# One projection of both branches, seven products per pair, in a stage of its own

## The chip, the cores and the metric

The kernel runs on one core of one Trainium2 chip. The metric is the device time of one execution in microseconds (us).

## The reference

`x` has 4096 rows of 1024 features. `h = RMSNorm(x)` goes through one projection (`w_in`, 1024 to 3072 columns). Its first 1024 columns feed the pooling branch: causal window means of 2, 4, 8 and 16 rows minus the value, mixed by a 128x128 matrix per group of 128 columns, times a SiLU gate. The other 2048 feed the attention branch: 8 heads of 64, chunks of 64 rows that each read themselves and eight chunks before, a relative-position bias, softmax, times a SiLU gate. Both branches (512 columns each) are concatenated; the part that the change rebuilds is

```
y = jnp.concatenate([y_pool, y_attn], axis=-1)
x = x + jnp.einsum('bse,ed->bsd', y, w_out[layer])
return rms_norm(x, final_norm_gain)
```

All tensors are float32. The kernel splits each operand of a product into a high and a low float16 part and makes three matmuls for one (high x high, high x low, low x high).

## The kernel before, in words

Rows are handled in 32 blocks of 128, in 16 pairs of 256 rows. One instruction stream per engine is written out by hand; each stream is in order, and `wait_ge` blocks everything behind it on that engine. SyncE (SP) issues almost all transfers from one such stream.

- **Stage 1** (`h_phase_*`): norm, transposes, and projection of values and gates. Most pairs are made with seven products of quarter matrices (Winograd's form of Strassen's scheme) in place of eight. The split operands of every pair go to memory (`h_ops`).
- **Stage 2** (`q_phase_*`): the pooling branch, 8 tiles `t` of 512 rows, each with 4 steps `k`; a step `m = 4t + k` is one window group and has 7 products of 12 matmuls of 256 columns (L1108 to L1111). VectorE (DVE) combines them (`take_*`, L1248), builds windows (`level`, L1307), and `scale_gate(m - 1)` (L1329, count `y_done`) makes the branch output of step m-1 during step m, after `take_c22(m)`. In the loop, ScalarE (ACT, `y_hi`) and GpSimd (POOL, `y_lo`) split it. TensorE (PE) then multiplies it with the pooling half of `w_out` (`output`, L1132) beside the next tile's products: 2, 2 and 4 outputs of 12 matmuls of 512 columns behind steps 1, 2 and 3. DVE adds `x` (`residual`, L1339), and SP stores the sum as `residual` in memory. `load_hop` (L1072) fetches the seven operands of tile t+1 into one buffer, each behind the wait for its last use in step 3 of tile t. `load_wk` (L1478) fetches pieces of the key and query weights; steps 8, 11, ..., 29 begin a piece, which POOL, ACT (L1207) and DVE (L1352) turn into operands. Outputs of the last tile stand in the passage to stage 3.
- **Stage 3** (`a_phase_*`): attention, 16 tiles of 256 rows, 8 heads each. Each head has three places (`other`, slots 3h to 3h+2) where PE does other work beside the softmax chain: slots 0 to 6 take query products of the tile to come, slots 7 to 16 the attention half of the output of tile t-1 (`output`, L1936), slots 17 to 23 key products (L1701 to L1704, 24 matmuls of 128 columns each). ACT makes exponentials (L2086) and high parts (L2092), POOL low parts (L2263). DVE adds the residual (L2192); ACT squares (L2101), POOL takes the root, DVE scales (L2201), SP stores the result.

Of the kernel before, what the change touches and what calls it, by code (L numbers as in the profile page):

```python
# [20 lines left out]
P = 128  # L21
# [84 lines left out]
def build(nc, x, norm_gain, w_in, pool_w, pool_scale, rel_fwd, rel_rev, w_out, final_gain, out):  # L106
# [7 lines left out]
    r_dram = nc.dram_tensor("residual", (BLOCKS, P, D), F32, kind="Internal").ap()  # L114
# [5 lines left out]
    with ctx:  # L120
# [58 lines left out]
        yp_h = view(Z, 19712, (2, NKT, PT), F16)  # L179
        yp_l = view(Z, 27904, (2, NKT, PT), F16)  # L180
        xres = view(E, 0, (2, D), F32)
        wot_h = view(E, 8192, (NKT, D), F16)
        wot_l = view(E, 16384, (NKT, D), F16)
# [11 lines left out]
        junk3 = view(RM, 40128, (D,), BF16)  # L195
# [4 lines left out]
        res = view(E, 0, (2, D), F32)  # L200
        res_last = view(RM, 43008, (2, D), F32)
        wob_h = view(E, 8192, (NKT, D), F16)
        wob_l = view(E, 16384, (NKT, D), F16)
# [8 lines left out]
        yT_h = view(Z, 34048, (NKT, AT), F16)  # L212
        yT_l = view(Z, 36096, (NKT, AT), F16)
# [697 lines left out]
        def h_phase_sp(sp):  # L911
# [86 lines left out]
        names = """psc_done mm p1_done u_done c11_done tanh_done z_done step_done y_done yh_done yl_done op_mm r_done  # L998
            wk_loaded wk_sums wk_hi wk_lo wot_hi wot_lo h_over""".split()
        Q = {n: sem("q_" + n) for n in names}  # L1000
        wot_loaded = [sem(f"q_wot_loaded{n}") for n in range(NKT)]
        entry_loaded = [sem(f"q_entry_loaded{s}") for s in range(PRODUCTS)]
        hop_loaded = [sem(f"q_hop_loaded{s}") for s in range(PRODUCTS)]
        xres_loaded = [sem(f"q_xres_loaded{s}") for s in range(2)]
        r_stored = [sem(f"q_r_stored{s}") for s in range(2)]

        pj6 = psum[0:6]
        op = [wide[:, 0:512], wide[:, 512:1024]]
        LASTM = GROUPS * PTILES - 1

        ENDBLK = PBLK * PTILES - 2

        def op_bank(n, n2):

            return psum[1 - n2][:, :] if n >= ENDBLK else op[n2]

# [36 lines left out]
        def wot_stage(n):  # L1053

            if n == 2:
                return wst2.rearrange("p a b c d -> p (a b c d)")
            return xres[:, min(n, 1), :]

# [16 lines left out]

        def wot_at(m):

            return {GROUPS: (0,), GROUPS + 1: (1, 2), GROUPS + 2: (3,)}.get(m, ())

        def q_phase_pe(pe):  # L1080
# [33 lines left out]
            def output(t, b, n2):  # L1114

                n = PBLK * t + b
                if b == 0 and n2 == 0:
                    pe.wait_ge(Q["yl_done"], GROUPS * t + GROUPS)
                    if t == 0:
                        pe.wait_ge(Q["wot_lo"], NKT)  # L1120
                        pe.wait_ge(H["t_done"], 4 * PAIRS)
                        pe.wait_ge(H["hlo_done"], 3 * PAIRS)
                        pe.wait_ge(H["b12_done"], b12_at(PAIRS - 1))
                if n == ENDBLK:
                    pe.wait_ge(A["kq_u"], 5 * 3)
                elif n > 0:
                    pe.wait_ge(Q["r_done"], 2 * n - 1 + n2)
                for kt in range(NKT):
                    yh = yp_h[:, t % 2, kt, b * P:(b + 1) * P]
                    yl = yp_l[:, t % 2, kt, b * P:(b + 1) * P]  # L1130
                    for part, w in ((yh, wot_h), (yh, wot_l), (yl, wot_h)):
                        mm = nc.tensor.matmul(op_bank(n, n2), part, w[:, kt, n2 * 512:(n2 + 1) * 512],  # L1132
                                              start=(kt == 0 and w is wot_h and part is yh),
                                              stop=(kt == NKT - 1 and part is yl))
                mm.then_inc(Q["op_mm"], 1)
# [11 lines left out]
            for b in range(2):  # L1147
                for n2 in range(2):
                    output(PTILES - 1, b, n2)
# [3 lines left out]
            for x in range(4):  # L1153
                first_maxima(pe, x)
                output(PTILES - 1, 2 + x // 2, x % 2)


        def outputs_after(t, k):

            if t == 0:  # L1160
                return ()
            if t == 1:
                return range(PBLK) if k == GROUPS - 1 else ()
            return ((), (0,), (1,), (2, 3))[k]

        def q_phase_act(act):
# [6 lines left out]
            def copy_c11(m):  # L1173
                act.wait_ge(Q["mm"], PRODUCTS * m + 5)
                at_least(act, Q["yl_done"], m - 1)
# [9 lines left out]

            def y_hi(m):
                t, k = m // GROUPS, m % GROUPS
                act.wait_ge(Q["y_done"], m + 1)
                if m == 0:
                    act.wait_ge(Q["h_over"], 1)  # L1190
                if k == 0 and t > 1:
                    act.wait_ge(Q["op_mm"], 2 * PBLK * (t - 1))
                nc.scalar.activation(yp_h[:, t % 2, GORDER[k], :], vb[:, m % 2, HIST:], ACT.Copy).then_inc(Q["yh_done"], 1)  # L1193

            def wot_hi(n):
                act.wait_ge(wot_loaded[n], 16)
                nc.scalar.activation(wot_h[:, n, :], wot_stage(n), ACT.Copy, scale=WS).then_inc(Q["wot_hi"], 1)
# [13 lines left out]
            for m in range(GROUPS * PTILES):  # L1211
                copy_p1(m)
                if m > 0:
                    gate_tanh(m - 1)
                for n in wot_at(m):
                    wot_hi(n)
# [4 lines left out]
                if m > 0:  # L1221
                    y_hi(m - 1)
            gate_tanh(LASTM)
            kq_copy_p1(act, 0)
            y_hi(LASTM)
# [9 lines left out]
        def q_phase_dve(dve):  # L1235
# [33 lines left out]
            def take_c12(m):  # L1269
                dve.wait_ge(Q["mm"], PRODUCTS * m + 6)  # L1270
                at_least(dve, Q["yl_done"], m - 1)
# [61 lines left out]
            def residual(t, b, n2):  # L1333

                n = PBLK * t + b
                dve.wait_ge(Q["op_mm"], 2 * n + n2 + 1)
                dve.wait_ge(xres_loaded[b % 2], 16 * (2 * t + b // 2 + 1))
                cols = slice(n2 * 512, (n2 + 1) * 512)
                nc.vector.scalar_tensor_tensor(  # L1339
                    out=xres[:, b % 2, cols], in0=op_bank(n, n2), scalar=1.0 / (WS * YS), in1=xres[:, b % 2, cols],  # L1340
                    op0=ALU.mult, op1=ALU.add).then_inc(Q["r_done"], 1)

            def wot_lo(n):
                dve.wait_ge(Q["wot_hi"], n + 1)
                nc.vector.scalar_tensor_tensor(
                    out=wot_l[:, n, :], in0=wot_stage(n), scalar=WS, in1=wot_h[:, n, :],
                    op0=ALU.mult, op1=ALU.subtract).then_inc(Q["wot_lo"], 1)

# [7 lines left out]
            for m in range(GROUPS * PTILES):  # L1356
# [16 lines left out]
                for n in wot_at(m):  # L1373
                    wot_lo(n)
# [8 lines left out]
                for b in outputs_after(t, k):  # L1383
                    for n2 in range(2):
                        residual(t - 1, b, n2)
# [1002 lines left out]
```

## Time and profile before

| | us |
|---|---|
| median of 3 runs (lowest, highest) | 1660.24 (1659.97, 1664.46) |
| profiled execution, device time | 1663.83 |
| its span | 1662.0 |
| TensorE busy | 1615.7 (97% of the span) |
| VectorE busy | 1064.2 (64%) |
| ScalarE busy | 839.0 (50%) |
| GpSimd busy | 667.6 (40%) |

Busy times are unions over an engine's overlapping instructions: a matmul of 512 columns is recorded with 379 ns, although the next one starts sooner. Pitch must therefore be read from starts. The mean granted clock of TensorE was 0.994 of full speed. Stage 1 ends at about 360 us, stage 2 at about 805 us, attention runs from about 857 us.

### The profile page before, as it was taken

What the parts mean: (1) busy time and instruction counts of PE and PEld (TensorE: products, weight loads), DVE (VectorE), ACT (ScalarE), POOL (GpSimd) and SP (SyncE); (2) the same over time, 40 slices, a digit from 0 to 9 for tenths busy, and PEclk for the clock granted to TensorE, in tenths of its full rate; (3) what the DMA queues carried; (4) which work ended last, traced back from release to release, by engine and by line L of the source; (5) the groups of instructions that cost most, each with busy time, mean ns of one, the idle gap of its engine ahead of it and who ended that gap; (6) DMA issues with size and microseconds to landing.
All of it is one profiled execution on the core that took longest, in us unless ns stands there. A gap on an engine that the chain in (4) does not pass through costs nothing. (4 is left out here: it accounts for less than half of the span.)

```text
span 1662.0 us, 44366 instructions
## 1 busy us (share of the span) xinstructions
PE 1615.7 (97%) x17944; PEld 1219.2 (73%) x17944; DVE 1064.2 (64%) x2201; ACT 839.0 (50%) x1589; POOL 667.6 (40%) x718
## 2 busy tenths in 40 slices
PE   7899999999999999999999999999999999999997
PEld 3455455468677777767778988889888898888974
DVE  7877767747565565556346666666666666666665
ACT  6555555522111111112126776767767676776775
POOL 3443333311101111111414465555655555555564
PEclk9999999999999999999999999999999999999999
DMA  6656456473615533542765534444344443344341
GB/s 238 211 188 222 183 210 222 178 264 136 221 61 177 199 127 105 178 165 90 224 210 165 154 90 136 138 135 146 96 131 140 135 142 114 117 137 137 96 141 51
DMA packets 144001, 258.01 MB, mean 155 GB/s; under 512 B 16024, under 2 KB 77992, under 8 KB 141752
## 3 DMA queue, kind: packets, MB, share of 16 engines
q1 hardware_dynamic: 142760, 253.88, 46.1%
q8 instruction: 143, 2.34, 0.6%
q0 software_dynamic: 1040, 1.31, 0.5%
q14 instruction: 58, 0.48, 0.1%
HBM read 151.40 MB, written 83.54 MB: 141 GB/s over the span
## 5 line engine op out<-in xcount | busy, mean ns | idle before, releaser
L2263 POOL TENSOR_TENSOR stages<-stages 128x512 f16<-128x512 f32 (+2 forms) x368 | 363.9, 991 | 353.9 <-ACT stages L2092 353.6
L1701 PE MATMUL bank<-middle,weights 128*128 128x128 f16 x1792 | 311.5, 219 | 2.7 <-DVE entry L1339 2.7
L1704 PE MATMUL bank<-middle,weights 128*128 128x128 f16 x1792 | 311.5, 219 | 0.0
L1703 PE MATMUL bank<-middle,weights 128*128 128x128 f16 x1792 | 311.4, 219 | 0.0
L2086 ACT ACTIVATE stages<-bank,log_ps 128x512 f32<-128x512 f32 (+2 forms) x368 | 221.6, 602 | 158.6 <-PE bank L1959 97.5
L1906 DVE CUSTOM_DVE_ANT_0 stages<-bank,stages 128x640 bf16<-128x640 f32 (+4 forms) x256 | 198.6, 776 | 74.6 <-PE bank L1871 74.3
L1108 PE MATMUL bank<-middle 128*128 128x256 f16 x784 | 214.4, 274 | 3.5 <-DVE stages L1248 3.5
L1111 PE MATMUL bank<-middle 128*128 128x256 f16 x784 | 214.5, 274 | 0.0
L1110 PE MATMUL bank<-middle 128*128 128x256 f16 x784 | 214.4, 274 | 0.0
L2092 ACT ACTIVATE stages<-stages 128x512 f16<-128x512 f32 (+2 forms) x368 | 202.9, 551 | 11.7
L1936 PE MATMUL bank<-entry,stages 128*128 128x512 f16 x768 | 190.8, 379 | 1.1 <-DVE stages L2148 1.1
L1701 PEld LDWEIGHTS bank<-middle,weights 128*128 128x128 f16 x1792 | 175.5, 98 | 3.4 <-issue 3.2
L1703 PEld LDWEIGHTS bank<-middle,weights 128*128 128x128 f16 x1792 | 175.6, 98 | 0.6
L1704 PEld LDWEIGHTS bank<-middle,weights 128*128 128x128 f16 x1792 | 175.5, 98 | 0.0
L1132 PE MATMUL bank<-entry,stages 128*128 128x512 f16 x768 | 169.7, 379 | 0.5 <-DVE middle L1734 0.5
L1956 PE MATMUL bank<-middle 128*128 128x256 f16 (+1 forms) x840 | 162.4, 243 | 3.1 <-DVE middle L2180 1.7
L1414 POOL TENSOR_TENSOR stages<-stages 128x512 f16<-128x512 f32 x32 | 38.0, 1189 | 302.3 <-ACT stages L1193 302.3
L330 PE MATMUL bank<-weights,middle 128*128 128x512 f16 x392 | 148.8, 380 | 1.1 <-DVE stages L689 1.1
L332 PE MATMUL bank<-weights,middle 128*128 128x512 f16 x392 | 148.8, 380 | 0.0
L333 PE MATMUL bank<-weights,middle 128*128 128x512 f16 x392 | 148.7, 379 | 0.0
L1132 PEld LDWEIGHTS bank<-entry,stages 128*128 128x128 f16 x768 | 75.0, 98 | 86.1 <-DVE middle L1734 0.6
L1734 DVE SCALAR_TENSOR_TENSOR middle<-bank,middle 128x256 f32<-128x256 f32 x160 | 67.8, 424 | 102.6 <-PE bank L1704 101.4
(157 smaller groups left out, 3673.1 us busy)
## 6 DMA issues: line engine op xcount, KB each, us to landing
entry<-in_x SPq DMA_DIRECT2D x64, 512.0 KB, 3.8
h_ops<-middle SPq DMA_DIRECT2D x16, 1792.0 KB, 6.1
middle<-h_ops SPq DMA_DIRECT2D x112, 256.0 KB, 5.5
middle<-h_ops SPq DMA_DIRECT2D x49, 512.0 KB, 7.6
middle<-middle SPq DMA_DIRECT2D x384, 64.0 KB, 2.0
residual<-entry SPq DMA_DIRECT2D x32, 512.0 KB, 2.9
out<-entry SPq DMA_DIRECT2D x32, 512.0 KB, 2.7
entry<-residual SPq DMA_DIRECT2D x30, 512.0 KB, 4.9
```

Source lines behind the costliest of these rows:

```text
L1108: nc.tensor.matmul(bank, wh, hop[:, :, s, 0, kt, :], start=(kt == 0 and s < 4), stop=False, skip_group_check=True)
L1110: nc.tensor.matmul(bank, wh, hop[:, :, s, 1, kt, :], start=False, stop=False, skip_group_check=True)
L1111: mm = nc.tensor.matmul(bank, wl, hop[:, :, s, 0, kt, :], start=False, stop=(kt == 3), skip_group_check=True)
L1132: mm = nc.tensor.matmul(op_bank(n, n2), part, w[:, kt, n2 * 512:(n2 + 1) * 512], start=(kt == 0 and w is wot_h and part is yh), stop=(kt = ...
L1701: nc.tensor.matmul(dst, wh, hop3[:, o, 0, kt, :], start=(kt == 0 and s < 2 and pair == 0), stop=False, skip_group_check=True)
L1703: nc.tensor.matmul(dst, wh, hop3[:, o, 1, kt, :], start=False, stop=False, skip_group_check=True)
L1704: mm = nc.tensor.matmul(dst, wl, hop3[:, o, 0, kt, :], start=False, stop=(kt == 3), skip_group_check=True)
L1906: nc.vector.tensor_tensor_reduce((junk0 if t == 0 and h < 2 else junk2)[:, c:640], wide[:, c:640], bias_q[:, h, c:640], 1.0, -3e38, ALU.ad ...
L1936: mm = nc.tensor.matmul(out_bank(t, i), yh, w, start=(m == 0), stop=(m == 11))
L2086: nc.scalar.activation(p32[g][:, a:b], score_bank(g)[:, a:b], ACT.Exp, bias=log_ps[:, 0:1]).then_inc(A["exp_done"], 1)
L2092: nc.scalar.activation(p_h[:, h % 2, c + a:c + b], p32[g][:, a:b], ACT.Copy).then_inc(A["ph_done"], 1)
L2263: nc.gpsimd.tensor_tensor(p_l[:, h % 2, c + a:c + b], p32[g][:, a:b], p_h[:, h % 2, c + a:c + b], ALU.subtract).then_inc(A["pl_done"], 1)
```

## The change

Neither branch is multiplied with `w_out` where it is made. Stage 2 stores each step's output to a new tensor `branches` in memory (`store_y`, on SP), and stage 3 stores the transposed attention output (`store_branch`). All `output`, `residual`, `y_hi`/`y_lo` and `r_dram` transfers go. The slots 7 to 16 stay empty; the key products move to slots 9, 11, ..., 21. A fourth stage (`f_phase_*`) loads each pair's branch outputs (1 MB) and x (1 MB) and makes the output with seven products, all in float16 pairs as before. Pairs 0 and 1 take the plain eight; half of these (16 halves of 6 matmuls) fill slots of the last two attention tiles, for which weights and branch outputs are loaded and split there.

```diff
 # stage 2, SP
+            def store_y(m):
+                sp.wait_ge(Q["y_done"], m + 1)
+                sp.dma_start(y_dram[2 * (m // GROUPS):2 * (m // GROUPS) + 2, :, GORDER[m % GROUPS], :].rearrange("a p n -> p a n"),
+                             vb[:, m % 2, HIST:].rearrange("p (a n) -> p a n", a=2)).then_inc(y_stored[m % 2], 16)
...
             for t in range(1, PTILES):
                 for k in range(GROUPS):
                     m = GROUPS * t + k
-                    if t == 1 and k == 1:
-                        load_res(0)
+                    store_y(m - 1)
                     if t == 1 and k == GROUPS - 1:
-                        load_res(1)
                         load_wk(0)
                     i, parts = wk_at(m)
                     if parts and parts[0] == 0 and i > 0:
                         load_wk(i)
                     if k == GROUPS - 1 and t + 1 < PTILES:
                         for s in range(PRODUCTS):
                             load_hop(sp, t + 1, s)
...
-                    for b in outputs_after(t, k):
-                        n = PBLK * (t - 1) + b
-                        store_res(n)
-                        load_res(n + 2)
+            store_y(LASTM)
             load_v(sp, 0, 0)
             load_gate(sp, 0, 0)
             load_bias(sp)
 # stage 2, PE
             for m in range(GROUPS * PTILES):
-                t, k = m // GROUPS, m % GROUPS
                 for s in range(PRODUCTS):
                     product(m, s)
-                for b in outputs_after(t, k):
-                    for n2 in range(2):
-                        output(t - 1, b, n2)
 # stage 3
+        K_SLOTS = (9, 11, 13, 15, 17, 19, 21)
...
-            first = 9 if t == 0 else 17
-            return (2 * t + 4, x - first) if t + 2 < ATILES and first <= x < first + PRODUCTS else None
+            return (2 * t + 4, K_SLOTS.index(x)) if t + 2 < ATILES and x in K_SLOTS else None
...
+        PLAIN_SLOTS = tuple((t, h, a) for t, h in [(LAST - 1, h) for h in (6, 7)] + [(LAST, h) for h in range(6)]
+                            for a in (0, 2))
+        WEIGHT_AT = {(LAST - 1, 3): (0,), (LAST - 1, 4): (1,), (LAST, 1): (2,), (LAST, 5): (3,)}
+        PLAIN_AT = {(LAST - 1, 4): ((0, 0),), (LAST - 1, 5): ((0, 1),), (LAST, 0): ((1, 0),), (LAST, 2): ((1, 1),)}
...
+            if p == 0 and half == 0:
+                sp.wait_ge(A["nat_lo"], 2 * ATILES)
+                for r in range(2):
+                    sp.wait_ge(yt_stored[r], 32)
+            else:
+                sp.wait_ge(F["plain_lo"], 2 * p + half)
+            sp.dma_start(ys[:, :, :], y_dram[p, :, NKT * half:NKT * half + NKT, :]).then_inc(F["ys_loaded"], 16)
...
                 move_k(sp, t + 1, 0)
                 move_q(sp, t + 1, 0)
                 load_v(sp, t + 1, 0)
                 load_gate(sp, t + 1, 0)
+                if t == LAST - 1:
+                    load_x4(sp, 0)
+                    for p, half in ((0, 0), (0, 1), (1, 0)):
+                        load_plain(sp, p, half)
                 move_k(sp, t + 1, 1)
                 move_q(sp, t + 1, 1)
 # stage 4, PE and VectorE
+            for p in range(PLAIN):
+                for q in range(4, 8):
+                    for part in range(2):
+                        plain_half(pe, p, q, part)
+            for p in range(PLAIN, PAIRS):
+                for s in range(PRODUCTS):
+                    product(p, s)
...
+            for p in range(PLAIN, PAIRS):
+                more = p + 1 < PAIRS
+                take_u2(p)
+                take_u4(p)
+                if more:
+                    operand_lo(p + 1, 0)
+                    operand_lo(p + 1, 1)
+                finish(2 * p - 2, 2 * p - 1)
+                take_c22(p)
+                if more:
+                    sums(p + 1)
+                finish(2 * p - 1, 2 * p)
+                add_x(p, 1, 0, 1, 2)
+                add_x(p, 0, 1, 1, 2)
+                take_c11(p)
+                if more:
+                    operand_lo(p + 1, 2)
+                take_c12(p)
+                take_c21(p)
```

## Rows read from the trace of the kernel before

**Rows 1.** The page, busy time by engine and share of the span

```profile
PE 1615.7 (97%) x17944; PEld 1219.2 (73%) x17944; DVE 1064.2 (64%) x2201; ACT 839.0 (50%) x1589; POOL 667.6 (40%) x718
```

**Rows 2.** The page, costliest groups: busy us, mean ns of one | idle before

```profile
L1936 PE MATMUL bank<-entry,stages 128*128 128x512 f16 x768 | 190.8, 379 | 1.1 <-DVE stages L2148 1.1
...
L1132 PE MATMUL bank<-entry,stages 128*128 128x512 f16 x768 | 169.7, 379 | 0.5 <-DVE middle L1734 0.5
```

**Rows 3.** Timeline of PE at 603 us: start us, us, instruction

```profile
602.71 5.34 PE L1132 MATMUL bank<-entry,stages 128*128 128x512 f16 x24
607.89 0.27 PE L1108 MATMUL bank<-middle 128*128 128x256 f16 x1
```

**Rows 4.** Timeline of SP at 612 us (step 19)

```profile
611.81 5.80 SPq L1072 DMA_DIRECT2D middle<-h_ops  x7
```

**Rows 5.** Timeline of DVE at 613 us (step 19)

```profile
613.67 0.74 DVE L1329 SCALAR_TENSOR_TENSOR stages<-stages,psc 128x512 f32<-128x512 f32 x1
```

**Rows 6.** L1072, the transfer issued at 554.0 us

```profile
DMA to landing us min/median/max: 4.6/4.6/4.6
```

**Rows 7.** L1072, the transfer issued at 498.3 us, behind two of L1478

```profile
DMA to landing us min/median/max: 5.9/5.9/5.9
```

**Rows 8.** L1072, the last of seven, issued at 559.4 us

```profile
DMA to landing us min/median/max: 8.4/8.4/8.4
```

**Rows 9.** Timeline of SP at 634 us (step 20)

```profile
633.91 0.91 SPq L1478 DMA_DIRECT2D entry<-in_w_in  x2
```

**Rows 10.** Timeline of ACT from 634 us (step 20)

```profile
634.17 0.38 ACT L1176 ACTIVATE stages<-bank 128x256 f32<-128x256 f32 x1 [4.34 <-PE bank L1111]
638.39 1.03 ACT L1207 ACTIVATE weights<-entry 128x256 f16<-128x256 f32 x3 [3.83 <-DMA entry<-in_w_in]
```

**Rows 11.** Timeline of PE at 646 us, in brackets its idle time before

```profile
646.34 0.28 PE L1108 MATMUL bank<-middle 128*128 128x256 f16 x1 [3.03 <-DVE stages L1248]
```

**Rows 12.** Stretch behind it: busy PE, PEld, DVE, ACT, POOL, then granted clock, DMA

```profile
646.00:650.00 4.00, 3.66 (x22) 2.62 (x23) 3.57 (x8) 0.63 (x1) 0.66 (x1) 0.67 0.02 4
```

**Rows 13.** Timeline of ACT in the passage to attention

```profile
806.46 0.38 ACT L1711 ACTIVATE middle<-bank 128x256 f32<-128x256 f32 x1 [10.30 <-PE bank L1704]
...
859.38 0.38 ACT L1711 ACTIVATE middle<-bank 128x256 f32<-128x256 f32 x1 [9.23 <-PE bank L1704]
```

**Rows 14.** Timeline of SP in the passage to attention

```profile
819.41 8.18 SPq L1821 DMA_DIRECT2D middle<-middle  x12
```

**Rows 15.** L1768, the transfer issued at 827.6 us

```profile
DMA to landing us min/median/max: 3.2/3.2/3.2
```

**Rows 16.** Timeline of ACT: first exponentials of heads (14,0), (14,6), (14,7), (15,0)

```profile
1555.96 0.47 ACT L2086 ACTIVATE stages<-bank,log_ps 128x256 f32<-128x256 f32 x1 [1.82 <-PE bank L1959]
...
1593.57 0.47 ACT L2086 ACTIVATE stages<-bank,log_ps 128x256 f32<-128x256 f32 x1
...
1597.59 0.46 ACT L2086 ACTIVATE stages<-bank,log_ps 128x256 f32<-128x256 f32 x1
...
1603.21 0.47 ACT L2086 ACTIVATE stages<-bank,log_ps 128x256 f32<-128x256 f32 x1 [1.67 <-PE bank L1959]
```

**Rows 17.** The page, DMA issues: KB each, median us to landing

```profile
entry<-in_x SPq DMA_DIRECT2D x64, 512.0 KB, 3.8
```

**Rows 18.** Groups by line: DVE's work on an output bank and on rows

```profile
L2192 DVE SCALAR_TENSOR_TENSOR entry<-bank,entry 128x512 f32<-128x512 f32 x60 | 41.4, 690 | 23.3 <-PE bank L1936 23.0
...
L2201 DVE SCALAR_TENSOR_TENSOR entry<-entry,stat 128x1024 f32<-128x1024 f32 x30 | 38.7, 1289 | 0.0
```

**Rows 19.** Timeline of DVE, two of L1307 without and two beside POOL

```profile
539.49 1.44 DVE L1307 TENSOR_TENSOR stages<-stages 128x525 f32<-128x525 f32 x2
...
582.54 1.84 DVE L1307 TENSOR_TENSOR stages<-stages 128x525 f32<-128x525 f32 x2
```

**Rows 20.** Timeline at the end: last PE group, ACT's last square

```profile
1649.64 4.05 PE L1936 MATMUL bank<-entry,stages 128*128 128x512 f16 x18
...
1655.69 1.06 ACT L2101 ACTIVATE middle<-middle 128x1024 bf16<-128x1024 f32 x1 [1.38 <-DVE middle L2192]
```

More of the change, by code:

```diff
@@ L1490, in q_phase_sp @@
             sp.nop().then_inc(Q["h_over"], 1)
-            for n in range(NKT):
-                load_wot(n)
+            for m in range(GROUPS - 1):
+                store_y(m)
             for t in range(1, PTILES):
@@ L2128, in head @@
                 if round_at(t, h):
-                    branch_hi(*round_at(t, h))
+                    branch_copy(*round_at(t, h))
                 other(t, h, 2)
-                for of, j in squares_at(t, h):
-                    square(of, j)
-                if t == 0 and h in WOB_HEADS:
-                    wob_hi(WOB_HEADS.index(h))
+                for w in WEIGHT_AT.get((t, h), ()):
+                    for half in range(2):
+                        final_hi(act, w, half)
+                for p, half in PLAIN_AT.get((t, h), ()):
+                    plain_hi(act, p, half)
             max_row(0, 0)
@@ L2139, in a_phase_act @@
                     head(t, h)
[L2140 to L2142 removed]
+            branch_copy(LAST, 1)
         def a_phase_dve(dve):
[L2145 to L2151 removed]
             def add_bias(t, h):
@@ L2216, in other @@
                         kq_take(dve, w, KQ_TAKES[s])
-                for of, i, _, end in output_slot(t, h, a):
-                    if end == 12:
-                        residual(of, i)
             def head(t, h):
@@ L2231, in head @@
                     maximum(dve, t2, h2, 1)
-                if round_at(t, h):
-                    branch_lo(*round_at(t, h))
                 other(t, h, 2)
-                for of, j in finish_at(t, h):
-                    finish(of, j)
-                if t == 0 and h in WOB_HEADS:
-                    wob_lo(WOB_HEADS.index(h))
+                before_h = (t, h - 1) if h > 0 else (t - 1, HEADS - 1)
+                for w in WEIGHT_AT.get(before_h, ()):
+                    for half in range(2):
+                        final_lo(dve, w, half)
+                for p, half in PLAIN_AT.get(before_h, ()):
+                    plain_lo(dve, p, half)
+                if (t, h) in TAKE_AT:
+                    plain_take(dve, *TAKE_AT[t, h])
             for t in range(ATILES):
@@ new lines, in final_source, with final_dst, final_hi @@
+        def final_source(w, half):
+            if w < 4:
+                return raw4[w][:, 2 * half:2 * half + 2, :]
+            return (s2w, s1w, s3w, s1w)[w - 4][half][:, :, :]
+        def final_dst(w, part, half):
+            return w4[2 if w == 7 else w][:, part, 2 * half:2 * half + 2, :]
+        def final_hi(act, w, half):
+            if w < 4:
+                act.wait_ge(raw_loaded[w], 16)
+                if w == 0 and half == 0:
+                    act.wait_ge(A["kq_mm"], PRODUCTS * 2 * ATILES)
+            elif w in (5, 6):
+                act.wait_ge(F["s13_done"], 2 * (w - 5) + half + 1)
+            else:
+                act.wait_ge(F["sum_done"], (2 if w == 7 else 0) + half + 1)
+            if w == 4 and half == 0:
+                act.wait_ge(A["pv_mm"], HEADS * ATILES)
+                act.wait_ge(A["max_done"], 2 * HEADS * ATILES)
+            if w == 7:
+                act.wait_ge(F["plain_mm"], 15)
+                act.wait_ge(F["w_lo"], 6)
+            nc.scalar.activation(final_dst(w, 0, half), final_source(w, half), ACT.Copy, scale=WS).then_inc(F["w_hi"], 1)
@@ L2344, in _ @@
             a_phase_pe(pe)
+            f_phase_pe(pe)
         @block.scalar
```

754 lines of the change are left out of this document (417 added, 337 removed).

## The prediction

> **What bounds the kernel now.** I read the page's busy times first: TensorE (PE) is busy for 1615.7 of 1662.0 us, VectorE (DVE) for 64%, the others for half or less [rows 1]. So PE's work sets the time, and removing matmuls pays if no wait takes their place. Then I read its groups. Both outputs are 768 matmuls each, recorded with 379 ns [rows 2]; that is duration, not pitch. The pitch is in the starts: 24 matmuls begin at 602.71 and the next product at 607.89, so 5.18 / 24 = 0.216 us [rows 3]. Last I read the SyncE (SP) queue and whoever waits for a transfer, since the change rebuilds that queue. Today's outputs are PE work that needs nothing fresh, so they also hide the landing of what comes next.
>
> **Matmuls.** Before: 1536. After: 2 pairs x 96 + 14 pairs x 84 = 1368. 168 fewer at 0.216 us are **-36 us**. Everything below is a wait that PE has beside that.
>
> **Stage 2, operands of the next tile.** A step has 84 matmuls of 256 columns, 1.31 us a product, 9.2 us a step. `load_hop` can only start behind the products of step 3, and product s of the next tile follows 7.9 us after the release of its buffer. Today four outputs (10.4 us) lie between. They go. SP must now also pass `store_y(m-1)` first, which waits for `y_done`: step 19 starts at 607.89 [rows 3], and L1329 ends at 613.67 + 0.74 = 614.41, 6.5 us into the step [rows 5]; before, the first load was out at 611.81, 3.9 us in [rows 4]. With the store's issue the load goes out at about 7.1 and lands 4.6 later [rows 6], at 11.7; PE wants it at 9.2. The others follow some 1.3 apart (the last of seven issued at 559.4 landed at 567.8 [rows 8]), so nothing is caught up: 2.7 us for step 19. In steps 7, 11 and 23 two weight transfers go out ahead (0.9 us of queue, landing after 5.9 [rows 7]): 8.05 + 5.9 = 13.95, 4.9 us each. Steps 15 and 27 follow a late step (next part); their `y_done` comes at about 12, and I count 4.4 each. Sum 2.7 + 3 x 4.9 + 2 x 4.4 = **+26**. Bounds: 6 x 2.5 = 15 to 6 x 6 = 36.
>
> **Stage 2, key and query weights.** Their pieces (steps 11 to 29, every third) today mostly go out at a step's start. Once, in step 20, SP was held up: ACT's copy after product 4 starts at 634.17, so the step began at about 627.5; the transfers went out at 633.91, 6.4 in [rows 9]; ACT could start on them at 638.39 [rows 10]; DVE, in order, was late for everything behind, and in the next step PE waited 3.03 us [rows 11]. After the change each of these transfers is behind `store_y`, at 6.9 to 8.4. Where a longer window keeps DVE busier I add its delay: steps 14, 17, 20, 26, 29: 3.7, 5.0, 3.5, 3.7, 5.0 = 20.9, less 3.3 that is there today: **+18** (in 11 and 23 the operand wait covers it). Bounds 5 x 2 - 3.3 = 7 to 25.
>
> **Clock.** After the 3.03 us of waiting the granted clock averages 0.67 over the next 4 us [rows 12]: it fell from 2.4 to 1.2 GHz for part of it, and some 1.7 us of work came later. Ten of the new waits are longer than that one: 10 x 1.7 = 17; part overlaps what PE would wait for anyway, so **+13** (0 to 20).
>
> **Passage to attention.** 96 output matmuls (20.7 us) leave it. Query products began at 806.46 and again at 859.38 [rows 13], some 52.5 us after PE's start on them. SP's order is now binding: key moves from 819.41 take 8.2 us of issue [rows 14], only then come the operands of tile 1, first landing 3.2 us later [rows 15]: 25.7 us after the start, when PE has had nothing since 18.7. Seven products (9.4) and the first maxima (about 5, with a lowered clock) make 41. So 11.5 us are gained of 20.7: **+9**, and +2 for the same wait ahead of tile 0's operands. Bounds 4 to 18.
>
> **Attention, tiles 1 to 13.** Outputs leave every tile (10.4 us). ACT needs about 4.0 us a head: head (14,6), which has no filling, lasts 1593.57 to 1597.59 [rows 16]. Tile 14 took 47.25 us with 7 products of filling; a full tile has 14, so about 51, after the change 41, or 5.1 a head; a thin head (one product) about 4.1. That just covers ACT. GpSimd and DVE have room. I count 0.6 us a tile, **+8**. Lower bound 0; upper 55: head (14,7), also unfilled, took 5.62 us [rows 16], and five or six thin heads at that length add 4 us a tile. The near row is the first, since key products were spread over the thin heads.
>
> **Tiles 14 and 15.** In tile 14 the filling is 4 half products (5.2 us) for 10.4 of outputs. But heads 3 to 5 are empty for PE, while ACT gets 2.1 us of weight splits twice and a branch split (L2101 shows 1.06 us for 1024 columns [rows 20]). The first branch transfer stands behind 12 moves at 0.68 us [rows 14], gate and value loads, and lands 3.8 us later [rows 17]: 15.5 us into head 3, ACT wants it at 12. The second waits for DVE's use of the only buffer, issued behind a head's other DVE work, and costs ACT about 6 us more. I get 57 us for the tile against 47.25 with 5 us less work: **+15** (0 to 22). What is late next is nothing in tile 15: its filling covers its ACT work.
>
> **Stage 4.** A pair is 84 matmuls, 18.1 us. DVE per pair: six takes at 0.69 [rows 18], ten half-width operations at about 0.68, two `finish` at 1.29 [rows 18]: 13.5. ACT and GpSimd need about 7 each, transfers are 3 MB. PE bounds it, and every product's bank and operand is ready several us early. Entry: the final attention transposes wait for DVE, and the clock may be down, **+3** (0 to 8). VectorE's weight sums (about 30 us) hide behind 20.7 us of plain halves and the first four products. Tail: from the last matmul at 1653.7 to the span's end are 8.3 us [rows 20]; after it take, square, root, a 1.29 us finish and a store are about 8: 0.
>
> A word on VectorE: beside GpSimd, two of its additions took 1.84 us instead of 1.44 [rows 19], so I add 0.2 us for some operations, hidden under 18.1. The Trainium skill ("SBUF — State Buffer", "Who interferes with whom") says more: with two SBUF inputs VectorE is fully blocked while GpSimd reads. The trace shows a smaller price; the rival below takes the rule.
>
> **Sum.** -36 + 26 + 18 + 13 + 11 + 8 + 15 + 3 = +58, on the span 1662.0: 1720. The profiled execution took 1663.8, the median 1660.2, 1.8 below its span: **1718**.
>
> **Rivals.**
> 1. *The queue keeps up and the gain survives.* If SP's wait costs nothing (branch output done before product 3), only passage and tiles 14, 15 lose: -36 + 9 + 15 = 1648. The waits need to stay below 31 us together. For it: PE is 97% busy now and nothing else is near its limit. Against it: 6.5 us in [rows 5] is fixed by product 3. This is the side I do not forecast: 0.12.
> 2. *Half of stage 2's waits.* Transfers land at their best, DVE catches up, the clock holds: 1718 - 9 - 10 - 13 = 1686. 0.14.
> 3. *Attention becomes ACT's and GpSimd's.* 5.6 us in each thin head, +55 in place of +8: 1765. For it the 5.62 of [rows 16]; against it the 4.0 there. 0.10.
> 4. *Stage 4 becomes VectorE's.* If GpSimd's four subtractions a pair block it outright, 13.5 + 4.8 = 18.3 > 18.1, with lateness for banks about 1 us a pair: 1732. The Trainium skill's rule would make it so; [rows 19] show 0.2 us an operation. 0.06.
>
> My own case: 0.58.
>
> **Range.** Unknown costs taken at their lower bounds give about 1665, at their upper (without rival 3) about 1750. I say 1662 to 1750. A measurement of this kernel can tell about 0.3% (5 us) from no change: faster 0.12, same 0.05 (between rivals 1 and 2), slower 0.83.
>
> **What would show it.** Right: in stage 2 PE waits of 2.5 to 5 us on `hop` transfers at each tile's first product and on DVE in the step after each weight transfer, L1072 issued 7 us into a step, granted clock at half behind them; a wait of some 7 us before the second set of key products; ACT waiting for `branches` in tile 14; stage 4 with PE full at 18.1 us a pair. Wrong: PE above 97% in stage 2, or thin heads above 5 us, or idle PE in stage 4.

## The result and the profile after

The changed kernel takes 1775.15 us (median of 4 runs, 1772.34 to 1779.77) where the kernel before took 1660.22 beside it: a ratio of 1.0689, 95% interval 1.0660 to 1.0717. It is slower by 115 us; I had forecast 58. The profiled execution took 1772.34 us, its span is 1770.6.

The busy line of the page after, and its row of granted clock in tenths:

```profile
PE 1616.6 (91%) x17776; PEld 1217.5 (69%) x17776; DVE 1165.0 (66%) x2290; ACT 894.9 (51%) x1680; POOL 748.1 (42%) x742
...
PEclk9999999999999999899999999999999788999999
```

TensorE is busy for as long as before (1615.7 in [rows 1]) although 168 matmuls are gone, and it is now 91% busy and not 97%. Both signs are bad: busy time that stays with less work points to work at a lower clock (the mean granted clock is 0.970 of full speed, where it was 0.994), and the other 154 us are idle. The view of waits says for whom TensorE stood (engine and line; whom it waited for; us in total, times, longest):

```profile
PE bank L1093 <- DMA middle<-h_ops: 23.5, 6, 4.6
PE bank L1525 <- DMA middle<-h_ops: 18.5, 3, 10.1
PE bank L262 <- DVE entry L644: 17.2, 8, 8.0
PE bank L1754 <- DVE middle L1937: 16.9, 29, 0.8
PE bank L1754 <- ACT stages L1866: 16.2, 27, 0.8
PE bank L1782 <- ACT stages L1866: 13.4, 5, 9.3
PE bank L1093 <- DVE stages L1175: 11.9, 6, 3.3
PE bank L1093 <- ACT stages L1121: 4.8, 1, 4.8
```

L1093 is stage 2's product, L1525 a key or query product, L1754 a head's scores, L1782 its values. L262 belongs to stage 1 and was there before. No single wait explains 115 us; rows 4 and 5 are fifty-six waits of 0.6 us. To place the loss I cut the span at ScalarE's landmarks (first copy of a stage 2 product, first copy of a key product, first exponential of each tile), and took away from the times of before what their output matmuls cost at 0.2157 us:

| stretch | before | before less outputs | after | lost |
|---|---|---|---|---|
| stage 2 | 444.2 | 299.2 | 352.3 | +53 |
| passage to attention | 54.4 | 33.7 | 48.1 | +14 |
| attention, tile 0 | 30.3 | 30.3 | 28.6 | -2 |
| tile 1 | 45.4 | 35.0 | 38.5 | +3 |
| tile 2 | 51.3 | 40.9 | 52.8 | +12 |
| tiles 3 to 13, each | 51.64 | 41.28 | 44.27 | +3.0 (11 x: +33) |
| tile 14 | 47.3 | 42.0 | 63.3 | +21 |
| tile 15 and entry of stage 4 | | 66.0 | 76.4 | +10 |

The last two rows of "before less outputs" also contain the plain products that the change puts there (5.2 us in tile 14), so that they compare with after. With 36 us for the removed matmuls the losses sum to +108, the difference of the spans (108.6). The windows of the same stretches (from:to, length, busy us of PE, PEld, DVE, ACT, POOL with instructions, granted clock, share of the DMA engines, GB/s), first of after, the last one of before:

```profile
362.20:714.50 352.30, 311.06 (x2705) 269.59 (x2703) 211.02 (x462) 58.99 (x155) 25.55 (x32) 0.95 0.36 124
714.50:762.50 48.00, 34.23 (x525) 33.32 (x523) 12.10 (x33) 6.46 (x12) 19.66 (x9) 0.83 0.71 178
1010.00:1054.30 44.30, 41.94 (x777) 40.54 (x778) 26.47 (x75) 34.15 (x64) 27.93 (x27) 1.00 0.42 115
1509.00:1753.00 244.00, 244.00 (x1132) 110.65 (x1131) 216.32 (x241) 89.09 (x159) 129.13 (x106) 1.00 0.44 168
```

```profile
1010.00:1061.60 51.60, 51.60 (x828) 45.11 (x825) 32.80 (x83) 36.41 (x69) 29.50 (x31) 1.00 0.42 130
```

Stage 2 has 41 us without a matmul, and its granted clock of 0.95 means some 35 us at the lower of its two levels, 1.2 for 2.4 GHz (0.05 x 2 x 352). An attention tile of before had TensorE full for all of its 51.60 us; after the change it stands for 2.4 of 44.3, at full clock. Stage 4 is full from end to end: there the change does what it says.

### The profile page after: what moved, and what is told of

Read it like the earlier page. It is cut to its first block and busy times, and to the rows that moved or that the text cites. A ratio compares the mean times of both kernels' runs of the same rounds, so it can differ in the third digit from the quotient of the medians.

```text
span 1770.6 us, 44380 instructions
## 1 busy us (share of the span) xinstructions
PE 1616.6 (91%) x17776; PEld 1217.5 (69%) x17776; DVE 1165.0 (66%) x2290; ACT 894.9 (51%) x1680; POOL 748.1 (42%) x742
## 5 line engine op out<-in xcount | busy, mean ns | idle before, releaser
L1525 PE MATMUL bank<-middle,weights 128*128 128x128 f16 x1792 | 315.4, 221 | 18.5 <-DMA middle<-h_ops 18.5
L1528 PE MATMUL bank<-middle,weights 128*128 128x128 f16 x1792 | 315.2, 221 | 0.0
L1527 PE MATMUL bank<-middle,weights 128*128 128x128 f16 x1792 | 315.2, 221 | 0.0
L1093 PE MATMUL bank<-middle 128*128 128x256 f16 x784 | 219.7, 280 | 35.4 <-DMA middle<-h_ops 23.5
L1095 PE MATMUL bank<-middle 128*128 128x256 f16 x784 | 219.6, 280 | 0.0
L1096 PE MATMUL bank<-middle 128*128 128x256 f16 x784 | 219.3, 280 | 0.0
L1754 PE MATMUL bank<-middle 128*128 128x256 f16 (+1 forms) x840 | 163.0, 243 | 34.9 <-DVE middle L1937 16.9
L1525 PEld LDWEIGHTS bank<-middle,weights 128*128 128x128 f16 x1792 | 176.9, 99 | 19.2 <-DMA middle<-h_ops 19.2
L1782 PE MATMUL bank<-middle,stages 128*128 128x65 f16 x1200 | 124.5, 194 | 18.1 <-ACT stages L1866 13.4
L1319 POOL TENSOR_TENSOR stages<-entry 128x256 f32<-128x256 f32 x8 | 5.8, 725 | 307.6 <-DMA entry<-in_w_in 307.6
L1757 PE MATMUL bank<-middle 65*128 65x128 f16 (+1 forms) x616 | 130.0, 243 | 0.0
L1175 DVE SCALAR_TENSOR_TENSOR stages<-bank,stages 128x256 f32<-128x256 f32 x160 | 67.2, 421 | 95.3 <-PE bank L1096 86.3
```

Of the source, the lines that this page charges most:

```text
L1093: nc.tensor.matmul(bank, wh, hop[:, :, s, 0, kt, :], start=(kt == 0 and s < 4), stop=False, skip_group_check=True)
L1095: nc.tensor.matmul(bank, wh, hop[:, :, s, 1, kt, :], start=False, stop=False, skip_group_check=True)
L1096: mm = nc.tensor.matmul(bank, wl, hop[:, :, s, 0, kt, :], start=False, stop=(kt == 3), skip_group_check=True)
L1525: nc.tensor.matmul(dst, wh, hop3[:, o, 0, kt, :], start=(kt == 0 and s < 2 and pair == 0), stop=False, skip_group_check=True)
L1527: nc.tensor.matmul(dst, wh, hop3[:, o, 1, kt, :], start=False, stop=False, skip_group_check=True)
L1528: mm = nc.tensor.matmul(dst, wl, hop3[:, o, 0, kt, :], start=False, stop=(kt == 3), skip_group_check=True)
```

## The experiments

Each is one edit of the changed kernel (one is an edit of the kernel before). "Off" is against 1775.15; ratios are to the kernel before, measured beside each run.

### Stage 2: the store of y behind the loads

```diff
                     m = GROUPS * t + k
-                    store_y(m - 1)
                     if t == 1 and k == GROUPS - 1:
                         load_wk(0)
...
+                    store_y(m - 1)
             store_y(LASTM)
```

> The only edit: in stage 2's loop on SP the store of the last step's y (it waits for ScalarE's second half of that step) is issued after the next w_k and hop-product loads and not ahead of them. Theory 'issue' (the loads land late because SP stands at y_done until the step before is almost over; the 23.5 us of PE waits for the hop tiles and the half-clock stretches that begin after them go with it): 35 to 45 us off 1775, that is 1730 to 1740, and PE L1093 <- DMA under 5 us. Rival 'landing' (one transfer of 512 KB behind another takes what it takes; the order on the queue is not what is late): 0 to 10 us off, PE L1093 <- DMA still about 20 us. The waits for DVE's take (11.9 us) should stay in both.

1726.03 us, 49 off, more than the 35 to 45 expected; ratio 1.0388 (1.0371 to 1.0405). Stage 2 takes 303.1 us for 352.3, four more than the 299.2 of its matmuls. Its window, and SP's queue at the end of the second tile, first in the changed kernel (start, length, line, transfer):

```profile
363.00:666.10 303.10, 296.26 (x2704) 263.31 (x2702) 214.27 (x462) 58.52 (x153) 32.56 (x32) 0.99 0.43 146
```

```profile
439.18 0.36 SPq L1347 DMA_DIRECT2D branches<-stages  x1
439.59 0.95 SPq L1356 DMA_DIRECT2D entry<-in_w_in  x2
440.59 4.16 SPq L1061 DMA_DIRECT2D middle<-h_ops  x7
```

and then in the experiment:

```profile
430.40 2.13 SPq L1356 DMA_DIRECT2D entry<-in_w_in  x2
433.53 1.69 SPq L1061 DMA_DIRECT2D middle<-h_ops  x2
```

The first of the seven loads goes out 6.4 us earlier in the step (6.4 us behind ScalarE's first copy in it before, at that copy now). TensorE has no wait for `h_ops` at L1093 any more, and the granted clock rises from 0.95 to 0.99. The waits for DVE at L1093 fall from 11.9 to 1.7, where I had expected them to stay: the weight transfers (L1356) stood behind the same store. So one line on a queue cost 49 us, of which the waits themselves were some 34: the rest is the half clock behind them. "Landing" is out as a cause of its own: the same seven transfers, in the same order among themselves, are in time. They also land sooner once they are not issued in one burst (the last section has the times).

### Attention: where the key products stand

```diff
-        K_SLOTS = (9, 11, 13, 15, 17, 19, 21)
+        K_SLOTS = (11, 14, 15, 17, 20, 21, 23)
```

> The only edit: in which slots of a pair the seven key products are put, (11, 14, 15, 17, 20, 21, 23) for (9, 11, 13, 15, 17, 19, 21), so that four of them stand where PE now has nothing between the end of a head's values and the scores of the next. Theory 'chain' (the 3.0 us that each attention tile loses are PE standing 0.59 us at a time for values, DVE's attend in the bank that both use, and then the next scores): 2 to 3 us less in each of some 12 tiles, 20 to 30 us off 1775. Rival 'throughput' (ScalarE's exponentials or GpSimd's half set the pace of a pair, and the waits only move): 0 to 3 us off, the same busy shares.

1762.71 us, 12 off; ratio 1.0602 (1.0578 to 1.0626). A tile takes 43.3 us for 44.3. That is between the two theories' numbers: the 0.6 us waits of scores for VectorE go, and in their place the values wait (L1782), for the exponentials (17.7 us in 19 waits, for 13.4 in 5) and 8 us more that the view puts down to nobody (10.8 us in 13 waits, for 2.7 in 1). A head has two such places, and seven products of 1.33 us can't fill ten. So I cut them:

```diff
+        K_HALVES = (10, 11, 12, 13, 14, 15, 16, 17, 18, 19, 20, 21, 22, 23)
...
+            if t + 2 < ATILES and x in K_HALVES:
+                n = K_HALVES.index(x)
+                return 2 * t + 4, n // 2, (n % 2,)
...
-                    for pair in range(2):
+                    for pair in pairs:
                         kq_half(pe, w // 2, 2 * (PRODUCTS * (w % 2) + s) + pair)
```

> The only edit: TensorE's 7 key products of a tile are cut into their 14 halves of 12 matmuls and put one each into slots 10 to 23, so that every slot of the heads 3 to 7 but one holds work; the takes of ScalarE and DVE stand where a product's second half is. Theory 'chain' (a head stands once for values, attend, next scores, and once for scores, exponential, values, some 0.6 to 0.7 us each; 0.67 us of work in the slot hides it): heads 3 to 7 take 23.0 us for 24.2, a tile 43.0 to 43.3, 12 to 16 us off 1775, no more than the other slots gave, since head 2 (5.8 us, one product in it) isn't touched. Rival 'throughput': 0 to 3 us.

1751.21 us, 24 off; ratio 1.0523 (1.0504 to 1.0542). A tile takes 42.4 us, better than the 43.0 to 43.3 that I expected. The same work, cut in halves, on unchanged other engines:

```profile
1010.00:1052.40 42.40, 41.81 (x780) 40.52 (x777) 26.20 (x75) 34.09 (x64) 27.83 (x27) 1.00 0.43 121
```

DVE, ACT and POOL are as busy as in the window of after at 1010 (26.2, 34.1 and 27.8 us) and TensorE's idle time falls from 2.4 to 0.6 us. "Throughput" is out for these 1.9 us of a tile's 3.0: no engine's pace set them, a chain of short steps from one engine to the next did. Head 2, which the edit doesn't touch, keeps its 5.81 us with one wait of 0.6 in it.

> As the run with the halves late, but the halves are in slots 7, 8, 10 to 14, 16 to 20, 22 and 23: the two empty slots of head 2 get one each, and three of the first slots of heads 3 to 7 are left empty. Theory 'chain': head 2 and the heads after it are then all at TensorE's own time, a tile takes 41.5 to 42.3 us, 24 to 33 us off 1775. Rival: in head 2 ScalarE and GpSimd are late because of the split of q in the same head, and head 2 keeps its 1.7 us of idle time: as the late halves, 12 to 16 us off, head 2 at 7.0 to 7.2 us.

The edit is K_HALVES = (7, 8, 10, 11, 12, 13, 14, 16, 17, 18, 19, 20, 22, 23). Inconclusive between its two theories, and slower than the late halves: 1758.07 us, 17 off; ratio 1.0567 (1.0551 to 1.0583). Head 2 takes 6.5 us in the mean of tiles 3 to 13, for 5.81, with 1.33 us more work in it, so it did have some 0.65 us to give, but TensorE then waits for the product's operands:

```profile
PE bank L1534 <- DMA middle<-h_ops: 32.9, 14, 11.0
```

That is 14.4 us more than with the late halves (18.5). Of it 3.4 us are in tile 2, most of the rest is one wait of some 0.8 us in each tile: slot 7 comes before the load for it has landed. Filling has to be ready, not only small.

### The removal alone, in the kernel before

```diff
-                for kt in range(NKT):
+                for kt in range(NKT - 1, NKT):
...
-                    for part, w in ((yh, wot_h), (yh, wot_l), (yl, wot_h)):
+                    for part, w in ((yl, wot_h),):
...
                 for m in range(first, end):
+                    if m < 11:
+                        continue
```

> The kernel before with 11 of the 12 matmuls of every output product left out, in stage 2 and in the attention stage, and everything else (copies, loads, stores, slots) as it was. What it leaves out is most of the multiplication by w_out. It asks what the removal alone gives. By the removed matmuls at 0.2157 us (theory 'PE-bound everywhere', which the prediction used): stage 2 from 444.2 to about 311, an attention tile from 51.64 to 42.2. Theory 'chain' says a tile keeps 2 to 3 us of that, 44.0 to 45.5, because in heads 3 to 7 the slots that held outputs are all but empty. Stage 2 has no store of y on SP here: if that store is the cause of its 53 us, this run shows 311 to 325; if it is the missing cover over the loads as such (what I had forecast), it shows 345 or more.

1498.61 us; ratio to the kernel before 0.9019 (0.9001 to 0.9036). A tile takes 45.7 us for 51.6: 5.9 us back for 44 matmuls that cost 9.5. The tile loses 3.6 us (a little more than "chain" allowed) with none of the other parts of the change in it, so most of the loss there comes from taking filling away and not from what was added. Head 2 takes 5.81 us here too. In stage 2 the number says "345 or more": the key products begin 87 us earlier, for 133 us of matmuls, so 357. But the waits say that the reason is another one:

```profile
PE bank L1132 <- DVE entry L1338: 23.8, 17, 8.2
...
PE bank L1108 <- DMA middle<-h_ops: 0.2, 1, 0.2
```

TensorE waits 23.8 us for VectorE's reading of the outputs, of which one matmul each is left and which still move x in and the sum out, and for the hop tiles (L1108) 0.2 us in all, against 23.5 in the changed kernel. The expectation's threshold was badly chosen, and stage 2 of this run decides little: its new waits stand where the outputs stood and give the loads time as the outputs did. What decides is the first experiment. There the outputs are gone as well and the loads are in time, so missing cover alone did not make the landing visible, the store ahead of the loads did.

### Three other places on SP's queue

```diff
+            sp.wait_ge(H["ext_stored"], 16)
+            for r, (dst, width) in enumerate(((bq_dram, 640), (bk_dram, 256))):
...
+            store_y(0)
             for s in range(PRODUCTS):
                 load_hop(sp, 1, s)
-            sp.wait_ge(H["ext_stored"], 16)
-            for r, (dst, width) in enumerate(((bq_dram, 640), (bk_dram, 256))):
...
+            for s in range(PRODUCTS):
+                load_hop3(sp, 1, s)
             for half in range(2):
                 move_k(sp, 0, half)
-            for s in range(PRODUCTS):
-                load_hop3(sp, 1, s)
...
-                    if t == 2:
-                        for i in range(3):
-                            load_raw(sp, i)
...
+                if 2 <= t < 5:
+                    load_raw(sp, t - 2)
```

> Three edits of the order on SP's queue, at three places far apart, each read from its own stretch. (a) Start of stage 2: the bias transfers and y's first store are issued ahead of the hop loads; theory: step 2's wait for ScalarE (4.8 us) and the half-clock time behind it go, 5 to 9 us; rival: the transfers then delay the hop loads by as much, 0. (b) Passage to attention: hop3(1) is loaded ahead of the moves of k; theory: the 10.1 us wait of PE for it goes, 8 to 10 us off the passage of 48.1; rival: the moves are then late instead, 0 or worse. (c) The three raw w_out loads of 1 MB are put one each in tiles 2, 3 and 4, behind their gate loads; theory: tile 2 falls from 52.8 to about 44.3 like its neighbours, 8 us; rival: the loss is spread over tiles 3 to 5. In all 20 to 27 us off by theory, 0 to 5 by the rivals.

1756.68 us, 18 off where the theories gave 20 to 27; ratio 1.0565 (1.0544 to 1.0585). (a) Stage 2 falls from 352.3 to 347.5: the ScalarE wait of the third step is gone (the pair of copies 14.8 us apart are now 5.2 apart). That place gained 7.9 us, of which 3.2 came back in later steps. (b) The passage falls from 48.1 to 43.6; a wait of 5.6 us for the same operands is left. (c) Tile 2 falls from 52.8 to 43.9, as theory said. Its cause in the changed kernel is plain on the queue: 3 MB of weights that nothing needs before tile 14 are ahead of the seven loads that tile 2 is waiting for.

```profile
842.98 1.60 SPq L2159 DMA_DIRECT2D entry<-in_w_out  x3
844.62 5.84 SPq L1592 DMA_DIRECT2D middle<-h_ops  x7
```

### Tile 14: the plain branches early

```diff
                 move_k(sp, t + 1, 0)
+                if t == LAST - 1:
+                    load_plain(sp, 0, 0)
                 move_q(sp, t + 1, 0)
...
+                    load_plain(sp, 0, 1)
                     load_x4(sp, 0)
-                    for p, half in ((0, 0), (0, 1), (1, 0)):
-                        load_plain(sp, p, half)
+                    load_plain(sp, 1, 0)
...
-                for p, half in PLAIN_AT.get(before_h, ()):
+                for p, half in PLAIN_AT.get((t, h), ()):
```

> The only edit: the first two loads of the plain branches are issued in tile 14 ahead of the x load of 1 MB and of q's move, and their subtraction on DVE is in the same head as before's copy. Theory 'queue' (ScalarE's two waits for the branches, 8.22 and 7.86 us, are the time that these loads stand behind x on the queue; with them goes the half clock of 27 us in tile 14): tile 14 from 63.3 to 48 to 53 us, 10 to 16 us off 1775. Rival 'memory' (the branches come late because their stores land late): ScalarE's waits stay, 0 to 3 us off. If q's move is then late, the first scores of tile 15 wait for it, 3 us back.

1761.32 us, 14 off; ratio 1.0598 (1.0580 to 1.0616). Tile 14 takes 49.6 us for 63.3. ScalarE's wait in the changed kernel and the two windows of that tile, of after and of this run:

```profile
ACT middle L2135 <- DMA middle<-branches: 16.1, 2, 8.2
...
1369.40:1432.70 63.30, 44.45 (x635) 37.12 (x633) 33.64 (x77) 39.28 (x70) 30.05 (x27) 0.78 0.31 93
```

```profile
1371.80:1421.40 49.60, 43.32 (x636) 36.80 (x633) 33.63 (x77) 39.33 (x69) 30.83 (x27) 0.86 0.40 119
```

The work on every engine is the same; what went is idle time, and part of the time at half clock. Q's late move cost nothing that I could see, but the next head of tile 15 in which DVE has a weight split, a branch split and a take one behind the other became 2 us longer (11.6 for 9.4).

### All of it together

The first version has the edits above with the early halves, hop3(1) moved further ahead (before the bias loads), and in the last tiles DVE's take of a plain product ahead of its splits:

```diff
+                if (t, h) in TAKE_AT:
+                    plain_take(dve, *TAKE_AT[t, h])
                 for w in WEIGHT_AT.get(before_h, ()):
```

> All the edits that gained, together: y's stores behind the loads, the bias transfers and y's first store ahead of the hop loads, hop3(1) ahead of both the bias loads and the moves of k, the raw w_out loads spread, the plain loads early, the halves in the early slots, and in the last tiles DVE's take of a plain product ahead of its weight split. If the parts add up (49, 5 to 9, 5 to 10, 9, 14, 24 to 33, and 3 to 5): 1650 to 1665, the time of the kernel before and its 36 us of saved matmuls still mostly spent in the start of the attention stage and in its last two tiles. If the waits that each part removes only hand over to one another: 1675 to 1690.

1671.66 us, 103 off; ratio 1.0048 (1.0033 to 1.0063). It misses my 1665 by 7. The passage shows why (L1702 are the first maxima):

```profile
PE bank L1535 <- DMA middle<-h_ops: 12.1, 13, 1.7
PE bank L1702 <- DMA middle<-middle: 9.9, 1, 9.9
```

Here hop3(1) is ahead of bias loads and moves, and the moves of k are now late for the maxima: the wait was handed on. The 13 waits at L1535 are the early halves' again.

The last version undoes what went wrong there:

```diff
+K_HALVES = (8, 11, 12, 13, 14, 15, 16, 17, 18, 19, 20, 21, 22, 23)
...
             for half in range(2):
                 move_k(sp, 0, half)
+            load_bias(sp)
...
+                if t == 5:
+                    load_fgain(sp)
...
-                    for half in range(2):
+                    for half in range(1 if w == 2 else 2):
                         final_lo(dve, w, half)
+                if (t, h) == (LAST, 4):
+                    final_lo(dve, 2, 1)
+                for p, half in PLAIN_AT.get((t, h) if t < LAST else before_h, ()):
```

> As the run with all edits together, with three of its places changed: halves in slots 8 and 11 to 23 (a tile 41.8 to 42.4 us for 42.8, some 6 to 9 us in all, since slot 7 waited for a hop load that had only just been issued); in the passage hop3(1), then k's moves, then the bias loads, and the final gain only in tile 5 (TensorE's 9.9 us wait for k's moves falls to 3 to 6, 4 to 6 us off); in the last tile DVE's half of the weight split is moved two heads back (3.3 us wait of the maxima goes, with its half clock 3 to 5 us). In all 1652 to 1660 for 1671.7, so faster than the kernel before by 0 to 0.6%. If the passage is bound by the bytes that it moves, its 44.8 us stay and the sum is 1656 to 1664.

1659.38 us (12 runs, 1657.39 to 1661.80) beside 1662.28 for the kernel before (17 runs); ratio 0.9984 (0.9975 to 0.9992). Its tiles take 42.4 us as with the late halves, so the slot in head 2 gave nothing more; the slow head of the last tile falls from 9.4 to 4.7 us (the last line of the edit, a fourth change which the expectation doesn't name, moves DVE's branch splits of that tile back to their old head, and it isn't shown which of the two did it); the passage takes 41.5 for 44.8, with this wait in it:

```profile
PE bank L1704 <- DMA middle<-middle: 7.6, 1, 7.6
```

It is the fastest version here, 0.2% below the kernel before (less than the 0.3% that I had called tellable, though the interval leaves 1 out), and 116 us faster than the changed kernel with the same arithmetic. Of its 36 us of removed matmuls 3 arrive (5 by the spans). Measured like the table above, the others are still spent in the passage (+8), in tiles 1 to 13 (+15, 1.1 a tile) and in tile 14 (+8), less 6 gained in stage 2 and tile 0; tile 15 and the entry of stage 4 have the rest (+6), which I did not take apart.

## Why the prediction was wrong

The direction was right, the size was half, and 1775 lies outside 1662 to 1750. The step that failed is **"Attention, tiles 1 to 13"**: +8 forecast, +48 measured. The other terms were 10 us short together on the spans (108.6 for 58). The rest of the distance from 1718 to 1775 is the step from span to median: 1.8 us less was forecast, 4.6 more measured.

- *Matmuls, -36*: right. Stage 4's 1176 matmuls take 253.6 us from first to last, 0.2157 each.
- *Stage 2, operands, +26*: 23.5 us of waits, six of them, at most 4.6. The cause, SP standing at `y_done` ahead of the loads, is shown by the first experiment. My first sentence on it ("they also hide the landing") gave missing cover equal weight; without the store the landing isn't waited for.
- *Stage 2, weights, +18*: 11.9 us of waits for DVE's take, inside 7 to 25.
- *Not forecast*: 4.8 us in the third step, where ScalarE's copy needs a buffer whose store stands on the queue behind loads and bias transfers.
- *Clock, +13*: what stage 2 lost beside those waits is 53 - 23.5 - 11.9 - 4.8 = 13. TensorE's busy time says the same: 311.1 us in the stage, against 296.3 for the same matmuls in the first experiment.
- *Passage, +11*: +14; one wait of 10.1 us at L1525 for hop3(1), behind the moves of k as said, and one of 1.0 for tile 0's operands, just ahead of the stretch.
- *Tiles 1 to 13, +8*: I compared totals, 4.1 us of TensorE's work in a thin head against 4.0 of ScalarE's, and took the larger. Both run at once only if neither waits for the other, and in a head they do, twice: scores, exponential, values; then values, VectorE's attend in the bank that both use, the next scores. One of these waits, in the changed kernel:

```profile
1009.95 0.27 PE L1754 MATMUL bank<-middle 128*128 128x256 f16 x1 [0.59 <-DVE middle L1937]
```

  Heads with one key product take 4.80, 4.74 and 4.86 us for the 4.1. Each of them, and head 2, has one such wait of 0.59, so four a tile, 2.4 of the 3.0 us that a tile lost (+33). That the gaps are the cause of at least 1.9 of these is shown by the halves, and that the additions aren't needed for the loss by the removal alone; of the last 1.1, 0.6 is head 2's gap and the rest is not taken apart. The row was in reach: an empty head, (14,6) in [rows 16], takes 4.02 us with its gaps open. A product of 1.33 put into a gap of 0.59 adds the 0.74 that doesn't fit: 4.76 (an estimate from these three numbers). I took the 4.0 for the time that ScalarE needs and the 4.1 for TensorE's, and neither is the head's. Key products were spread over the thin heads, but one to a head, and a head has two gaps. The other 15: in tile 2 (+12) w_out's three loads cost 9 (52.8 us, and 43.9 when they are spread), 3 MB that my account of the queue left out altogether though it counted every move. The 3 left there, and tile 1's +3, are the size of the other tiles' loss; the halves took tile 1 from 38.5 to 36.9.
- *Tiles 14 and 15, +15 and 0*: tile 14 lost 21, the two branch waits (8.2 and 7.9) with more half clock than I had allowed (27 us in one piece). *Entry, +3*: tile 15 and the entry lost 10.
- *Stage 4*: the time was right, the reading of VectorE was not. TensorE is busy for 244.00 of 244.00 us, so rival 4's time (1732) did not come. Its mechanism did:

```profile
1615.30 1.67 POOL L2447 TENSOR_TENSOR middle<-middle 128x512 f16<-128x512 f32 x1 [2.33 <-ACT middle L2240]
1615.27 0.68 DVE L2330 TENSOR_TENSOR middle<-middle 128x512 f32<-128x512 f32 x1
1615.87 1.65 DVE L2333 TENSOR_TENSOR middle<-middle 128x512 f32<-128x512 f32 x1
1617.44 2.18 DVE L2392 SCALAR_TENSOR_TENSOR weights<-weights,stat,entry 128x1024 f32<-128x1024 f32 x1
```

  L2330 began just before GpSimd's subtraction and took 0.68 us. L2333, the same operation, began inside it, took 1.65 and ended at 1617.52, 0.55 behind the subtraction's end (1616.97). The next one, a `finish`, took 2.18 us beside GpSimd's second subtraction, where without one it takes 1.28. In all 13 pairs that have them, such operations of 512 columns end 0.55 us behind the subtraction they met and the `finish` 1.08. By the rule of the Trainium skill that rival 4 took ("SBUF — State Buffer", "Who interferes with whom") a VectorE instruction with two SBUF inputs and a GpSimd instruction that reads SBUF exclude each other. The trace agrees. Four operations a pair are held up so, 3.8 us in all, near the rival's 4.8; VectorE is busy for 16.2 of a pair's 18.2 us, where I had 13.5: that is 13.5 + 3.8, less some 1.1 because each operation starts 0.08 us before the one ahead of it ends. So it stays under TensorE, with 2 us to spare. The 0.2 us an operation that I read from [rows 19] was no price: there GpSimd's operation began inside the first of the two additions, so only the second waited, and only for what was left of it (it ended at 584.38, 0.56 behind GpSimd's 583.82):

```profile
582.77 1.05 POOL L1425 TENSOR_TENSOR stages<-entry 128x256 f32<-128x256 f32 x1 [3.67 <-DMA entry<-in_w_in]
```

- *Rival 3* gave nearly the right time (1765) by the wrong mechanism: it made ScalarE and GpSimd the pace of a head, and 24 us came back without taking any work from them. At 0.10 it lay outside the range; a bound that I had written down as reachable (+55) should have been in it. Nor are 1665 and 1750 the sums of my bounds: those give about 1650 and, with attention left at +8, 1761.

## What to carry to other kernels

Matmuls that wait for nothing are worth more than their time where the rest of a stage is a chain between engines: removing them gives back their time less every gap that they covered, so count the gaps of one iteration (here two a head, one of them left open at 0.6 us in half of the heads) and not the totals of its engines. If the filling shrinks, cut it into as many pieces as there are gaps, and put each where its operands have landed. On a queue that works in order, a wait costs what stands behind it: a store that waits for the end of a step belongs behind the loads of the next, and a megabyte that nobody needs yet doesn't belong ahead of them.

## What the runs showed of the hardware

- A wait costs more than its length. In stage 2 the experiment that took away some 34 us of waits, of up to 4.6 us each, gave 49; the granted clock of that stage rose from 0.95 to 0.99. In attention, waits of 0.6 us, fifty-six of them, left it at 1.00.
- A VectorE operation with both inputs in SBUF stands still while GpSimd reads SBUF: 1.65 us for 0.68, and 2.18 for 1.28, each ending behind the end of GpSimd's subtraction. One that reads a PSUM bank does not: in stage 2 of the kernel before, the takes at L1248 took 0.42 us beside GpSimd as without it.
- A small transfer can be late because of what is ahead of it on its queue: y's first store, 256 KB, which at that line lands after 2.4 us in the median, landed after 15.3 us. Ahead of it were seven loads of 512 KB and the two DRAM to DRAM bias transfers, issued up to 17 us before. With the bias transfers still ahead but the loads behind it, it landed after 6.8.
- Loads of 512 KB land later when they are issued in one burst. In the changed kernel the last seven of stage 2 went out within 3.7 us and landed after 5.4 (the first) to 10.9 us (the last). In the first experiment, where they went out some 1.3 us apart, it was 3.5 to 6.5.
